# Hybrid decoder trunk with a hierarchical MoE: 16 KB weight rows, the head sums in a row, combines in four banks

## The chip, the cores and the metric

The kernel runs on one NeuronCore of one Trainium2 chip. The metric is the device time of one execution in microseconds (us). Engines are named as the profile names them: PE (matmuls; PEld is its weight load), DVE, ACT, POOL, and SP, which issues the DMAs.

## What is computed

The reference is a two-layer trunk on 512 tokens of width 1024, all in float32. Layer 0 mixes tokens with sliding-window attention (8 query heads, 2 key/value heads of 64) beside a gated delta rule; layer 1 with retention. After each follows a mixture of experts: 32 experts, each token goes to 2 of one group's 8.

```python
def attn_delta_mixer(h, pos, w_in, ...):
    aq, ak, av, bqkv, bz, ba, bb = _split(h @ w_in, EVEN_SPLITS)
    q = rms_norm(aq.reshape(bsz, s, SWA_Q_HEADS, SWA_HEAD_DIM), q_gain)
    k = rms_norm(ak.reshape(bsz, s, SWA_KV_HEADS, SWA_HEAD_DIM), k_gain)
    y_a = sliding_window_attention(partial_rope(q, pos), partial_rope(k, pos), v, sinks)
...
def expert_block(args):                       # in hierarchical_moe
    xb, e = args
    hid = jax.nn.silu(xb @ w_gate[e]) * (xb @ w_up[e])
    return hid @ w_down[e]
...
for layer in range(DEPTH):
    x = x + mixer(rms_norm(x, ...), ...)      # attn_delta_mixer, then retention_mixer
    x = x + hierarchical_moe(rms_norm(x, ln_ffn[layer]), ...)
```

w_gate and w_up of an expert are 1024 x 512, w_down is 512 x 1024: 2 MB each, 6 MB for an expert, and every expert's weights are read in both layers.

## The kernel before, in words

Each engine's program is written out by hand, and engines wait for each other by semaphores. The residual stream X stays in SBUF as 4 tiles of 128 tokens. PSUM is used as eight banks of 128 x 512 float32, PB[0] to PB[7]. Weights pass through a ring of six slots of 2 MB.

**Attention, in layer 0.** `attn_pe` computes the projections, then four products for the delta rule's first head and one for its second (`gproj_pe`, n = 0 to 4, 24 matmuls each), which need the weights split into an upper and a lower part; POOL makes the lower part for n = 0 to 3, DVE (`split_gdn_lower`, L422) for n = 4, after the loop that follows. In `attn_dve` DVE goes through the four token tiles: it sums the squares of every head (L597), waits for POOL, which makes rstd of it (L570, L571 in `attn_pool`), and then scales and rotates q and k of that tile (L605 to L615). In the second tile it also copies the convolution's weights (L600) and clears three columns (L603), for which ACT waits at L694. The four rotated tiles are then transposed on PE (L467).

**Experts.** Experts are taken in pairs, 16 pairs a layer, 64 token slots for each expert of a pair, so that the two work in the two halves of PE's columns. For pair i the six slots hold gate, up and down of both experts; `experts_sp` loads each matrix of the next pair as soon as PE has used up the one before it (L2102). In `experts_pe` pair(i) does this work, in this order:

- gate(i) and up(i): 64 matmul records at L1712, into PB[0] and PB[1];
- combine(i - 1): the rows of the pair before are brought back to the tokens, as eight sums of 128 x 512 (m = 0 to 7), two matmuls each (L1730), each added to X on DVE (L2014). The sums go into BC, PB[6] and PB[7], in turn;
- gather(i + 1): the tokens of the next pair are picked by a one-hot product (L1683), 8 matmuls for each half, into PB[0] and PB[1];
- hidden_t(i): four transposes (L1717) of the product of SiLU(gate) and up, which DVE makes at L1742 when up is done;
- x_transposed(i + 1): four transposes for each half (L1688), and slots_transposed(i + 1), four more (L1697);
- down(i): 32 matmul records at L1723, into BY, PB[4] and PB[5]. ACT and DVE take them out as an upper and a lower part (L1735, L1739).

combine is cut into four pieces of two sums between the others. A sum may start when the add of the sum two before it is done:

```python
                    if not (is_at(i, 0) and m < 2):
                        pe.wait_ge(*mw("added", 8 * i + m - 1))
                    comb_mm(pe, comb_bank(m), m, b).then_inc(ms("comb"), 1)
```

Pairs 2 to 13 are a loop in the program, pairs 0, 1, 14 and 15 are written out. The last pair's sums go through all eight banks (`LAST_ORDER`) and are added at L2019. On DVE pair(i) makes one-hots, the hidden product, six adds, x_out(0) (L1692, which takes the transposed tokens out of PSUM), two adds, x_out(1), and the lower part of y.

Of the kernel before, what the change touches and what calls it, by code (L numbers as in the profile page):

```python
# [26 lines left out]
NT = SEQ // P  # L27
# [3 lines left out]
RING = 6  # L31
# [62 lines left out]
def program(nc, x, ln_mix_even, w_in_even, conv_w_even, a_log_even, dt_bias_even, q_gain_even, k_gain_even,  # L94
# [8 lines left out]
    with ctx:  # L103
# [469 lines left out]
        def attn_dve(dve, step):  # L573
# [18 lines left out]
            for t in range(NT):  # L592
                v = QKv[:, t, :].rearrange("p (h d) -> p h d", d=ADH)
                x1, x2 = v[:, :, 0:8], v[:, :, 8:16]
                rot = [rt[:, a, t * 80:(t + 1) * 80].rearrange("p (h d) -> p h d", d=8) for a in range(4)]
                dve.wait_ge(sg("a_sq"), t + 1)
                dve.tensor_reduce(a_ss[:, t * AQK:(t + 1) * AQK], sq_tmp[:, t, :].rearrange("p (h d) -> p h d", d=ADH), AX, ALU.add).then_inc(sg("a_sums"), 1)  # L597
                if t == 1:
                    dve.wait_ge(sg("d_cw"), 1)
                    dve.tensor_copy(cw, PB[2][:, 0:48]).then_inc(sg("d_conv_ready"), 1)  # L600
                    dve.wait_ge(sg("d_conv_ready"), 1)
                    dve.wait_ge(sg("a_proj"), 8)
                    dve.memset(xc[:, :, 0:3], 0.0).then_inc(sg("d_conv_ready"), 1)  # L603
                dve.wait_ge(sg("a_rstd"), t + 1)
# [1055 lines left out]
        def comb_bank(m):  # L1660

            return BC[m % 2]

# [107 lines left out]
        def experts_pe(pe, l):  # L1771
# [21 lines left out]
            def down(i):  # L1793
                for u in range(2):
                    pe.wait_ge(*w_need(l, 4 + u, i))
                if not is_at(i, 0):
                    pe.wait_ge(*mw("y_lower", 2 * i))
                pe.wait_ge(*mw("ht_out", i + 1))
                for half in range(2):
                    down_mm(pe, half, range(2), w_two(l, 4, 4)).then_inc(ms("y"), 1)  # L1800

            def combine(i, b, ms_):
                for m in ms_:
                    if m == 0:
                        pe.wait_ge(*mw("y_lower", 2 * i + 2))
                        pe.wait_ge(*mw("ot_out", i + 1))
                    if not (is_at(i, 0) and m < 2):
                        pe.wait_ge(*mw("added", 8 * i + m - 1))
                    comb_mm(pe, comb_bank(m), m, b).then_inc(ms("comb"), 1)
# [23 lines left out]
            def pair(i, b):  # L1833
# [4 lines left out]
                if before:  # L1838
                    combine(i - 1, 1 - b, (0, 1))
                if more:  # L1840
                    gather(i + 1, 0)
                hidden_t(i)
                if before:
                    combine(i - 1, 1 - b, (2, 3))
                if more:
                    gather(i + 1, 1)
                if before:
                    combine(i - 1, 1 - b, (4, 5))
                if more:
                    x_transposed(i + 1, 0)  # L1850
                if before:
                    combine(i - 1, 1 - b, (6, 7))
                if more:
                    slots_transposed(i + 1)
                    x_transposed(i + 1, 1)
# [115 lines left out]
        def experts_dve(dve, l, step):  # L1971
# [54 lines left out]
            def pair(i, b):  # L2026
# [11 lines left out]
                hidden(i, b)  # L2038
                adds(i - 1, range(6))
                if more:  # L2040
                    x_out(i + 1, 0)
                adds(i - 1, (6, 7))
                if more:
                    x_out(i + 1, 1)
# [50 lines left out]
        def experts_sp(sp, l):  # L2095
            mats = (w_gate[l], w_up[l], w_down[l])

            def load(i, q):
                c = c_moe[l] + q
                sp.wait_ge(*(released[c - RING] if is_at(i, 0) else freed(l, q, i)))  # L2100
                src = mats[q // 2].rearrange("e (p k) n -> p e (k n)", p=P)[:, one(2 * i + q % 2), :]
                sp.dma_start(slot_of(c), src.rearrange("p e n -> p (e n)"), max_dma_last_dim=4096).then_inc(w_landed[c % RING], 16)  # L2102

# [6 lines left out]
        def overflow_sp(sp, l):  # L2110
# [4 lines left out]
            with sp.If(n_most > SLOTS):  # L2115
                sp.wait_ge(*mw("y", NE))
                with sp.Fori(1, SEQ // SLOTS) as b:
                    with sp.Fori(0, PAIRS) as i:
                        n = (b - 1) * PAIRS + i
                        for q, name in enumerate(("v_g0", "v_g1", "v_u0", "v_u1", "v_y0", "v_y1")):  # L2120
                            src = (w_gate[l], w_up[l], w_down[l])[q // 2].rearrange("e (p k) n -> p e (k n)", p=P)[:, bass.ds(2 * i + q % 2, 1), :]
                            sp.dma_start(w_over(l), src.rearrange("p e n -> p (e n)"), max_dma_last_dim=4096).then_inc(ms("v_w"), 16)
                            sp.wait_ge(*over_wait(l, name, n))
# [513 lines left out]
```

## Time and profile before

| | |
|---|---|
| median of 3 runs | 1770.93 us (1770.86 to 1772.2) |
| the profiled execution | 1770.01 us, its span 1768.1 us |
| PE busy | 1730.7 us, 98% |
| DVE, ACT, POOL busy | 659.0 (37%), 444.8 (25%), 212.2 us (12%) |
| read from HBM | 457 MB, 260 GB/s over the span |
| DMA in the experts' slices | 408 to 410 GB/s |
| experts, layer 0 and layer 1 | about 341 to 839 us and 1267 to 1765 us |
| chain of waits: PE, DVE, DMA | 91%, 3%, 2% |

PE's busy time in this profile covers the time in which matmuls follow one another with modelled ends, so 98% doesn't say that each matmul runs at its shortest. The chain of waits says what each stretch was spent on; the windows say what the DMA engines moved in it.

### The profile page before, as it was taken

The page shows a single profiled execution, that of the slowest core. Times are in us where ns is not written, and L with a number is a line of the kernel's source. Part 1 is how long each engine was busy: PE and PEld are TensorE (multiplying, and loading weights), DVE is VectorE, ACT ScalarE, POOL GpSimd, SP SyncE. Part 2 cuts the span into 40 slices and gives each one's busy share as a digit, 9 for nine tenths or more (in the row PEclk, how much of TensorE's full clock was granted, in tenths as well). Part 3 has the DMA queues.
Part 4 walks back from the last instruction along what each step waited for, and adds up shares of the span by engine and source line. Part 5 has one row for each costly group of instructions (what it writes and reads, how often), then busy time and mean ns, then how long its engine had stood idle before and what let it go on. Part 6 is the DMA issues. An engine that isn't in the chain of part 4 may idle for free.

```text
span 1768.1 us, 23453 instructions
## 1 busy us (share of the span) xinstructions
PE 1730.7 (98%) x9323; PEld 1106.5 (63%) x9323; DVE 659.0 (37%) x1164; ACT 444.8 (25%) x868; POOL 212.2 (12%) x152
## 2 busy tenths in 40 slices
PE   7899999999999999999999999999999999999998
PEld 6778988754444545454988888888754544445453
DVE  3775764423232323234413223132522332323233
ACT  4365653311111111112342322323311111111110
POOL 2400100100000000001533442442000000000000
PEclk9999999999999999999999999999999999999999
DMA  8410112599999999999122222122499999999996
GB/s 196 100 48 1 49 51 96 189 408 409 409 409 410 409 410 409 410 409 364 49 72 83 84 95 96 48 96 95 191 393 409 410 409 410 410 410 409 410 409 243
DMA packets 141177, 460.39 MB, mean 260 GB/s; under 512 B 5552, under 2 KB 31376, under 8 KB 140208
## 3 DMA queue, kind: packets, MB, share of 16 engines
q1 hardware_dynamic: 140368, 457.01, 66.5%
q0 software_dynamic: 736, 2.34, 1.1%
q8 instruction: 54, 0.88, 0.2%
q14 instruction: 19, 0.16, 0.0%
HBM read 457.24 MB, written 2.10 MB: 260 GB/s over the span
## 4 chain that ended last, share of the span: by engine, by line
PE 91%; DVE 3%; DMA 2%; ACT 1%; SPq 1%; issue 1%; POOL 0%; DVEq 0%; ACTq 0%
PE bank L153 28%; PE bank L1712 25%; PE bank L1723 12%; PE bank L1730 7%; PE bank L1683 7%; PE bank L1688 2%; DMA ring<-in_w_in_even_dram 1%; PE bank L2240 1%; DMA ring<-in_w_in_odd_dram 1%; PE bank L1717 1%; SPq L2487 1%; PE bank L1478 1%; PE bank L1697 1%; PE bank L927 1%; PE bank L914 1%
## 5 line engine op out<-in xcount | busy, mean ns | idle before, releaser
L1712 PE MATMUL bank<-ring,SCR 128*64 128x512 f32 x2048 | 448.9, 593 | 1.6 <-DVE SCR L1692 0.9
L153 PE MATMUL bank<-ring_r 128*128 128x512 f32 (+2 forms) x1216 | 359.8, 378 | 10.0 <-DVE ring_r L422 5.1
L1712 PEld LDWEIGHTS bank<-ring,SCR 128*64 128x64 f32 x2048 | 152.6, 137 | 291.6 <-issue 284.5
L153 PEld LDWEIGHTS bank<-ring_r 128*128 128x128 f32 x1216 | 225.5, 192 | 52.2 <-DVE ring_r L422 5.5
L2171 POOL TENSOR_TENSOR ring_r<-ring,ring_r 128x1024 fp32r<-128x1024 f32 x62 | 150.7, 2463 | 707.2 <-DVE ring_r L2171 482.7
L1723 PE MATMUL bank<-ring,SCR 128*64 128x512 f32 x1024 | 226.8, 595 | 0.0
L2014 DVE TENSOR_TENSOR X<-X,bank 128x512 f32<-128x512 f32 x240 | 153.9, 682 | 96.1 <-PE bank L1730 96.0
L1742 DVE SCALAR_TENSOR_TENSOR SCR<-SCR,bank 128x512 f32<-128x512 f32 x32 | 23.9, 748 | 360.8 <-PE bank L1712 360.8
L1730 PE MATMUL bank<-SCR_r 128*128 128x512 f32 x512 | 152.5, 419 | 1.6 <-DVE SCR_r L1739 0.9
L1723 PEld LDWEIGHTS bank<-ring,SCR 128*64 128x64 f32 x1024 | 70.6, 137 | 132.3 <-issue 128.7
L153 PE MATMUL bank<-ring_r,SCR_r 128*128 128x512 f32 x576 | 138.7, 395 | 0.0
L1919 ACT COPY SCR<-bank 128x512 f32<-128x512 f32 x64 | 37.5, 587 | 352.8 <-PE bank L1683 352.8
L153 PE MATMUL bank<-ring_r,HT_r 128*128 128x512 f32 (+1 forms) x320 | 121.3, 379 | 0.0
L1730 PEld LDWEIGHTS bank<-SCR_r 128*128 128x128 f32 x512 | 86.4, 189 | 54.3 <-issue 25.1
L153 PEld LDWEIGHTS bank<-ring_r,SCR_r 128*128 128x128 f32 x576 | 106.5, 188 | 22.0
L1739 DVE TENSOR_TENSOR SCR_r<-bank,SCR_r 128x512 fp32r<-128x512 f32 x64 | 44.3, 692 | 194.9 <-ACT SCR_r L1735 194.9
L153 PE MATMUL bank<-HT_r,ring_r 128*128 128x512 f32 (+1 forms) x288 | 107.6, 374 | 0.0
L2164 ACT CAST ring_r<-ring 128x1024 fp32r<-128x1024 f32 x64 | 62.4, 1050 | 96.2 <-PE bank L153 89.4
L1735 ACT CAST SCR_r<-bank 128x512 fp32r<-128x512 f32 x64 | 37.5, 585 | 195.3 <-PE bank L1723 195.3
L1683 PE MATMUL bank<-HT_r,SCR_r 128*128 128x512 f32 x256 | 69.8, 394 | 0.0
L1939 ACT ACTIVATE SCR<-bank 128x512 f32<-128x512 f32 x32 | 19.1, 597 | 199.5 <-PE bank L1712 199.5
L1683 PE MATMUL bank<-XN_r,SCR_r 128*128 128x512 f32 x256 | 68.7, 390 | 0.0
(413 smaller groups left out, 1710.0 us busy)
## 6 DMA issues: line engine op xcount, KB each, us to landing
ring<-in_w_gate_dram SPq DMA_DIRECT2D x64, 2048.0 KB, 15.1
ring<-in_w_up_dram SPq DMA_DIRECT2D x64, 2048.0 KB, 18.4
ring<-in_w_down_dram SPq DMA_DIRECT2D x64, 2048.0 KB, 15.3
ring<-in_w_in_odd_dram SPq DMA_DIRECT2D x8, 2048.0 KB, 8.9
ring<-in_w_in_even_dram SPq DMA_DIRECT2D x16, 512.0 KB, 6.7
ring<-in_w_in_odd_dram SPq DMA_DIRECT2D x8, 1024.0 KB, 8.0
ring<-in_w_out_odd_dram SPq DMA_DIRECT2D x4, 2048.0 KB, 7.5
ring<-in_w_out_even_dram SPq DMA_DIRECT2D x2, 2048.0 KB, 8.2
```

Source lines behind the costliest of these rows:

```text
L153: mm = pe.matmul(out, lhs[a], rhs[b], start=(first and i == 0), stop=(last and i == 2))
L1683: mm = pe.matmul(BX[half][:, :], OH[:, t, :], part[:, t, half * 512:(half + 1) * 512], start=(t + i == 0), stop=(t == NT - 1 and i == 1))
L1688: mm = pe.transpose(BX[g][:, j * P:(j + 1) * P], XG[:, g * 512 + j:(g + 1) * 512:4], ident)
L1712: mm = pe.matmul(bank[SLOTS * u:SLOTS * u + SLOTS, :], x_tile(k, u), w[u][:, k, :], start=(k == 0), stop=(k == KT - 1))
L1723: mm = pe.matmul(BY[half][SLOTS * u:SLOTS * u + SLOTS, :], HHT[:, j * P + SLOTS * u:j * P + SLOTS * u + SLOTS], w[u][:, j, half * 512:(hal ...
L1730: mm = pe.matmul(bank[:, :], OT[b][:, t * P:(t + 1) * P], part[:, half * 512:(half + 1) * 512], start=(i == 0), stop=(i == 1))
L1735: return act.copy(YU[:, half * 512:(half + 1) * 512], BY[half][:, :])
L1739: return dve.tensor_tensor(YL[o], BY[half][:, :], YU[o].bitcast(F32), ALU.subtract)
L1919: act.copy(XG[:, half * 512:(half + 1) * 512], BX[half][:, :]).then_inc(ms("xg"), 1)
L2014: dve.tensor_tensor(x_part(m), x_part(m), comb_bank(m)[:, :], ALU.add).then_inc(ms("added"), 1)
L2164: act.copy(WU[j % 2][:, at], slot_of(c)[:, at]).then_inc(sg("r_upper"), 1)
L2171: eng.tensor_tensor(ring_r[:, c % RING, at], slot_of(c)[:, at], WU[j % 2][:, at].bitcast(F32), ALU.subtract).then_inc(sg("r_lower"), 1)
```

## The change

Three edits.

1. The experts' weight loads no longer say `max_dma_last_dim=4096`. A load is 128 rows of 16 KB, which was cut into elements of 4 KB and is now moved as 16 KB elements.
2. In `attn_dve` the four sums of squares stand in a row, with the copy and the clearing behind them, and the scaling and rotation of the four tiles follow in a second loop.
3. In the experts the sums go through four banks, PB[6], PB[7], PB[4], PB[5]; a sum waits for the add of the sum four before it, and down waits for the adds of sums 6 and 7, as it writes PB[4] and PB[5]. The sums are done in two pieces of four. The twelve transposes for the next pair stand together ahead of down. On DVE the eight adds stand together ahead of both x_out.

```diff
             for t in range(NT):
-                v = QKv[:, t, :].rearrange("p (h d) -> p h d", d=ADH)
...
                 dve.wait_ge(sg("a_sq"), t + 1)
                 dve.tensor_reduce(a_ss[:, t * AQK:(t + 1) * AQK], sq_tmp[:, t, :].rearrange("p (h d) -> p h d", d=ADH), AX, ALU.add).then_inc(sg("a_sums"), 1)
                 if t == 1:
                     dve.wait_ge(sg("d_cw"), 1)
                     dve.tensor_copy(cw, PB[2][:, 0:48]).then_inc(sg("d_conv_ready"), 1)
-                    dve.wait_ge(sg("d_conv_ready"), 1)
-                    dve.wait_ge(sg("a_proj"), 8)
-                    dve.memset(xc[:, :, 0:3], 0.0).then_inc(sg("d_conv_ready"), 1)
+            dve.wait_ge(sg("d_conv_ready"), 1)
+            dve.wait_ge(sg("a_proj"), 8)
+            dve.memset(xc[:, :, 0:3], 0.0).then_inc(sg("d_conv_ready"), 1)
+            for t in range(NT):
+                v = QKv[:, t, :].rearrange("p (h d) -> p h d", d=ADH)
...
                 dve.wait_ge(sg("a_rstd"), t + 1)
                 step.then(dve.tensor_tensor(v, v, a_rs[...], ALU.mult))
...
         def comb_bank(m):
-            return BC[m % 2]
+            return (BC + BY)[m % 4]
...
                 for half in range(2):
+                    if not is_at(i, 0):
+                        pe.wait_ge(*mw("added", 8 * i - 1 + half))
                     down_mm(pe, half, range(2), w_two(l, 4, 4)).then_inc(ms("y"), 1)
...
-                    if not (is_at(i, 0) and m < 2):
-                        pe.wait_ge(*mw("added", 8 * i + m - 1))
+                    if not (is_at(i, 0) and m < 4):
+                        pe.wait_ge(*mw("added", 8 * i + m - 3))
                     comb_mm(pe, comb_bank(m), m, b).then_inc(ms("comb"), 1)
...
                 if before:
-                    combine(i - 1, 1 - b, (0, 1))
+                    combine(i - 1, 1 - b, range(4))
                 if more:
                     gather(i + 1, 0)
                 hidden_t(i)
-                if before:
-                    combine(i - 1, 1 - b, (2, 3))
                 if more:
                     gather(i + 1, 1)
                 if before:
-                    combine(i - 1, 1 - b, (4, 5))
+                    combine(i - 1, 1 - b, range(4, 8))
                 if more:
                     x_transposed(i + 1, 0)
-                if before:
-                    combine(i - 1, 1 - b, (6, 7))
-                if more:
                     slots_transposed(i + 1)
                     x_transposed(i + 1, 1)
                 down(i)
...
                 hidden(i, b)
-                adds(i - 1, range(6))
+                adds(i - 1, range(8))
                 if more:
                     x_out(i + 1, 0)
-                adds(i - 1, (6, 7))
-                if more:
                     x_out(i + 1, 1)
                 y_out(i)
...
-                sp.dma_start(slot_of(c), src.rearrange("p e n -> p (e n)"), max_dma_last_dim=4096).then_inc(w_landed[c % RING], 16)
+                sp.dma_start(slot_of(c), src.rearrange("p e n -> p (e n)")).then_inc(w_landed[c % RING], 16)
```

**PE, pair 1 of layer 0, from up's end to down.** L1712 is gate and up, L1730 the sums, L1683 the gather, L1717 hidden_t, L1688 and L1697 the transposes for the next pair, L1723 down. Before:

```order
L1730 MATMUL bank<-SCR_r 128x512 x4
L1683 MATMUL bank<-HT_r,SCR_r 128x512 x4
L1683 MATMUL bank<-XN_r,SCR_r 128x512 x4
L1717 MATMUL bank<-CE,SCR 128x128 x4
L1730 MATMUL bank<-SCR_r 128x512 x4
L1683 MATMUL bank<-HT_r,SCR_r 128x512 x4
L1683 MATMUL bank<-XN_r,SCR_r 128x512 x4
L1730 MATMUL bank<-SCR_r 128x512 x4
L1688 MATMUL bank<-CE,SCR 128x128 x4
L1730 MATMUL bank<-SCR_r 128x512 x4
L1697 MATMUL bank<-CE,SCR 128x128 x4
L1688 MATMUL bank<-CE,SCR 128x128 x4
```

And with the change, in which each of these lines has a number one higher:

```order
L1731 MATMUL bank<-SCR_r 128x512 x8
L1684 MATMUL bank<-HT_r,SCR_r 128x512 x4
L1684 MATMUL bank<-XN_r,SCR_r 128x512 x4
L1718 MATMUL bank<-CE,SCR 128x128 x4
L1684 MATMUL bank<-HT_r,SCR_r 128x512 x4
L1684 MATMUL bank<-XN_r,SCR_r 128x512 x4
L1731 MATMUL bank<-SCR_r 128x512 x8
L1689 MATMUL bank<-CE,SCR 128x128 x4
L1698 MATMUL bank<-CE,SCR 128x128 x4
L1689 MATMUL bank<-CE,SCR 128x128 x4
```

The same 16 matmuls of the sums now stand in two groups of 8 in place of four of 4, and nothing of them stands between the transposes.

**SP, the load of one pair in the loop of layer 0.** Before:

```order
L2102 DMA ring<-in_w_gate_dram 128x4x1024
L2102 ISA
L2102 DMA ring<-in_w_gate_dram 128x4x1024
L2102 DMA ring<-in_w_up_dram 128x4x1024 x2
L2102 DMA ring<-in_w_down_dram 128x4x1024 x2
```

With the change:

```order
L2098 DMA ring<-in_w_gate_dram 128x4096
L2098 ISA
L2098 DMA ring<-in_w_gate_dram 128x4096
L2098 DMA ring<-in_w_up_dram 128x4096 x2
L2098 DMA ring<-in_w_down_dram 128x4096 x2
```

The same six loads in the same places, each with 128 elements of 4096 floats in place of 512 of 1024.

**DVE, layer 0's attention, from the first sum on.** Before, one tile's turn and the next sum stand like this (the sum is L597):

```order
L605 TENSOR_TENSOR SCR<-SCR 128x640
L606 TENSOR_TENSOR SCR<-SCR 128x640
L609 TENSOR_TENSOR SCR<-SCR,CE 128x80
L610 TENSOR_TENSOR SCR<-SCR,CE 128x80
L611 TENSOR_TENSOR SCR<-SCR,CE 128x80
L612 TENSOR_TENSOR SCR<-SCR,CE 128x80
L614 TENSOR_TENSOR SCR<-SCR 128x10x8
L615 TENSOR_TENSOR SCR<-SCR 128x10x8
L597 TENSOR_REDUCE SCR<-SCR 128x10
L600 COPY SCR<-bank 128x48
L603 MEMSET ring 128x3x3
```

With the change, the sums (L594) stand ahead of the first tile's turn:

```order
L597 COPY SCR<-bank 128x48
L594 TENSOR_REDUCE SCR<-SCR 128x10 x2
L600 MEMSET ring 128x3x3
L606 TENSOR_TENSOR SCR<-SCR 128x640
L607 TENSOR_TENSOR SCR<-SCR 128x640
```

No sum stands between two tiles' turns any more, and no tile's turn stands between a sum and the next.

## Rows read from the trace of the kernel before

**Rows 1.** The page's chain of waits, by engine.

```profile
PE 91%; DVE 3%; DMA 2%; ACT 1%; SPq 1%; issue 1%; POOL 0%; DVEq 0%; ACTq 0%
```

**Rows 2.** Chain of waits in time: gates of pairs 1, 10, 15, layer 1's 1, 15.

```profile
375.18 13.73 PE bank L1712 x64
...
650.59 13.95 PE bank L1712 x64
...
804.10 6.89 PE bank L1712 x32
...
1301.41 13.73 PE bank L1712 x64
...
1729.97 6.87 PE bank L1712 x32
```

**Rows 3.** Windows: us; PE, PEld, DVE, ACT, POOL busy; PE clock, DMA share, GB/s.

```profile
500.00:550.00 50.00, 50.00 (x235) 25.72 (x232) 14.84 (x25) 6.38 (x12) 0.00 (x0) 1.00 1.03 410
```

**Rows 4.** DMA issues of a window from 527 us: size in KB, us to landing.

```profile
ring<-in_w_up_dram SPq DMA_DIRECT2D x2, 2048.0 KB, 20.7
```

**Rows 5.** Windows, while one load of w_out_odd, 128 rows of 16 KB, runs.

```profile
1174.00:1178.00 4.00, 4.00 (x20) 3.30 (x19) 3.97 (x4) 2.25 (x3) 4.00 (x3) 1.00 1.01 430
```

**Rows 6.** The page's DMA issues: KB, us from issue to landing.

```profile
ring<-in_w_out_odd_dram SPq DMA_DIRECT2D x4, 2048.0 KB, 7.5
```

**Rows 7.** Chain of waits in time, one pair (3) of layer 0: start, us, what.

```profile
436.12 13.73 PE bank L1712 x64
449.85 1.12 PE bank L1730 x4
...
453.29 0.93 PE bank L1730 x4
...
456.05 0.91 PE bank L1730 x4
...
457.43 1.27 PE bank L1730 x4
...
466.63 13.73 PE bank L1712 x64
```

**Rows 8.** The same view, pair 0 of layer 0, which has no sums.

```profile
364.88 1.85 PE bank L1683 x8
```

**Rows 9.** PE and DVE in order of time: the first sums of a pair.

```profile
603.03 1.20 PE L1730 MATMUL bank<-SCR_r 128*128 128x512 f32 x4
...
603.90 1.28 DVE L2014 TENSOR_TENSOR X<-X,bank 128x512 f32<-128x512 f32 x2
```

**Rows 10.** Chain of waits in time, last pair of layer 1; then DVE there.

```profile
1743.99 1.13 PE bank L1730 x4
...
1749.90 7.04 PE bank L1723 x32
...
1744.80 1.28 DVE L2014 TENSOR_TENSOR X<-X,bank 128x512 f32<-128x512 f32 x2
```

**Rows 11.** Attention: PE in order of time, then the chain of waits in time.

```profile
77.97 0.80 PE L153 MATMUL bank<-ring_r 128*128 128x512 f32 x1 [5.06 <-DVE ring_r L422]
...
77.97 8.32 PE bank L153 x24
...
133.56 5.54 PE bank L153 x24
```

**Rows 12.** Windows in that stretch (columns as in rows 3).

```profile
80.00:82.00 2.00, 2.00 (x7) 1.54 (x6) 2.00 (x3) 0.00 (x0) 0.00 (x0) 0.50 1.20 272
```

**Rows 13.** DVE in order of time, attention: second tile, third sum and turn.

```profile
61.69 0.82 DVE L605 TENSOR_TENSOR SCR<-SCR 128x640 f32<-128x640 f32 x1 [2.14 <-POOL SCR L571]
...
64.45 0.81 DVE L597 TENSOR_REDUCE SCR<-SCR 128x10 f32<-128x640 f32 x1
...
67.63 0.82 DVE L605 TENSOR_TENSOR SCR<-SCR 128x640 f32<-128x640 f32 x1 [2.37 <-POOL SCR L571]
```

**Rows 14.** ACT in order of time at the end of layer 0's experts.

```profile
827.74 1.99 ACT L2164 CAST ring_r<-ring 128x1024 fp32r<-128x1024 f32 x2 [6.75 <-DMA ring<-in_w_in_odd_dram]
```

More of the change, by code:

```diff
@@ L592, in attn_dve @@
             for t in range(NT):
-                v = QKv[:, t, :].rearrange("p (h d) -> p h d", d=ADH)
-                x1, x2 = v[:, :, 0:8], v[:, :, 8:16]
-                rot = [rt[:, a, t * 80:(t + 1) * 80].rearrange("p (h d) -> p h d", d=8) for a in range(4)]
                 dve.wait_ge(sg("a_sq"), t + 1)
@@ L600, in attn_dve @@
                     dve.tensor_copy(cw, PB[2][:, 0:48]).then_inc(sg("d_conv_ready"), 1)
-                    dve.wait_ge(sg("d_conv_ready"), 1)
-                    dve.wait_ge(sg("a_proj"), 8)
-                    dve.memset(xc[:, :, 0:3], 0.0).then_inc(sg("d_conv_ready"), 1)
+            dve.wait_ge(sg("d_conv_ready"), 1)
[3 more added lines that the diff above has]
+                v = QKv[:, t, :].rearrange("p (h d) -> p h d", d=ADH)
+                x1, x2 = v[:, :, 0:8], v[:, :, 8:16]
+                rot = [rt[:, a, t * 80:(t + 1) * 80].rearrange("p (h d) -> p h d", d=8) for a in range(4)]
                 dve.wait_ge(sg("a_rstd"), t + 1)
@@ L2121, in overflow_sp @@
                             src = (w_gate[l], w_up[l], w_down[l])[q // 2].rearrange("e (p k) n -> p e (k n)", p=P)[:, bass.ds(2 * i + q % 2, 1), :]
-                            sp.dma_start(w_over(l), src.rearrange("p e n -> p (e n)"), max_dma_last_dim=4096).then_inc(ms("v_w"), 16)
+                            sp.dma_start(w_over(l), src.rearrange("p e n -> p (e n)")).then_inc(ms("v_w"), 16)
                             sp.wait_ge(*over_wait(l, name, n))
```

## The prediction

> **What bounds the kernel now.** I read the chain of waits first. It is PE for 91% [rows 1], so time is won only where PE is held up or where its own sequence gets shorter. Both happen in two places: the experts, 28 nearly equal pairs, and one gap in the attention.
>
> In the experts the starts of the gates give a pair's length. From pair 1 to pair 15 layer 0 takes 804.10 - 375.18 = 428.92 us, layer 1 1729.97 - 1301.41 = 428.56 us [rows 2]: 857.5 us for 28 pairs, 30.62 each. They aren't all alike. In the middle gate and up take 13.95 us and a pair (804.10 - 650.59) / 5 = 30.70; at the start of a layer gate and up take 13.73 [rows 2]. The difference of 0.22 us is a wait for weights. A pair needs six loads of 2,097,152 bytes, 12.58 MB; in 30.70 us that is 410 GB/s, and the windows show a flat 410 with the DMA engines' share at 1.03 [rows 3]. The up weights take 20.7 us from issue to landing [rows 4], where a load alone takes 7.5 [rows 6]: PE is a little faster than the stream, and the queue's delay has grown until PE stops for it, at the start of up. So PE and DMA are within 1% of each other: speeding up either alone meets the other at once.
>
> A pair that doesn't wait for DMA is, piece by piece [rows 7]: gate and up 13.73, sums 1.12 + 0.93 + 0.91 + 1.27 = 4.23, and the rest (gathers, transposes, down) unchanged below. Such a pair lasts 466.63 - 436.12 = 30.51 us.
>
> In the attention PE stands still for 5.06 us ahead of the product n = 4, whose lower weights DVE makes at L422 [rows 11]. The 24 matmuls behind the gap take 8.32 us; the same 24 later take 5.54 [rows 11]. In that stretch the granted clock is 0.50, the lower level of 1.2 GHz [rows 12]; it fell in PE's gap. DVE comes late to L422 as it waits in each of four tiles for POOL's rstd: 2.14 and 2.37 us idle in the two tiles shown, and as much in the others [rows 13].
>
> **The 16 KB elements.** Six loads, same bytes, same places. What 16 KB elements give is bounded by two rows: the present stream, 410 [rows 3], as the case in which nothing changes, and the 430 GB/s of a load of w_out_odd, which is moved so already [rows 5]. I take 430, as it is the same kind of load on the same queue; then the stream needs 12.58 MB / 430 = 29.3 us for a pair. PE needs more than that (next part), so all waits for weights in the pairs go, about 0.2 us in each pair of the second half of a layer, and the stream has 0.9 us to spare. Below nothing: a load of this kind alone takes 7.5 us to land [rows 6], of which 4.9 are movement; this would hurt if it weren't overlapped with the next (a rival).
>
> The Trainium skill, DMA: Bandwidth & Descriptors, section Specifications, says that transfers of 512 B and more run at line rate. By that rule 4 KB elements lose nothing, and this edit gives 0; rows 3 and 5, 410 against 430, speak against it, though the second is one load at a time. The same page's fabric ceiling of 435 GB/s leaves room for 430.
>
> **The sums, in two groups of 8.** In a row of matmuls of this kind four cost 0.91 us, 0.2275 each [rows 7]. First group, after up: 1.12 + 0.91 = 2.03. Second group, after the gather: 8 x 0.2275 = 1.82. Together 3.85 against 4.23: 0.38 less, most of it the wait for an add in the last group (1.27 against 0.91). The gather that now follows hidden_t costs 0.03 more (1.85 after transposes in pair 0 [rows 8], against 1.82). I take 0.35: a pair of 30.51 - 0.35 = 30.16 us. Bounds: 30.51 (the switch costs only move) and 30.0 (switches cheaper than read).
>
> The new waits. Sum 4 waits for the add of sum 0. DVE's adds start 0.87 us after the first group (603.90 against 603.03, where PE starts it) and take 0.64 each [rows 9]: the four are done at 3.4, and the second group starts only at 2.03 + 1.82 + 1.85 and 0.5 of hidden_t, at 6.2. Down waits for the add of sum 6. With the same delay from a group's start to its first add, adds 4 to 6 are done by 6.2 + 0.87 + 3 x 0.64 = 9.0; down is reached at 6.2 + 1.82 and 1.4 of transposes (the rest of the pair: 466.63 - 457.43 - 1.27 is 7.9 with only two of the three), at 9.4. That is 0.4 us to spare, thin, but down's second half, which needs add 7 (9.6), comes 3.5 us later. x_out ends near 11.0 and the next gate is at 16.4; nobody waits for it. Neither wait costs anything as long as adds take 0.64.
>
> 28 pairs: 857.5 - 28 x 30.16 = 857.5 - 844.5 = **13.0 us**.
>
> **The last pair of each layer** has no gathers to hide adds, and takes 1749.90 - 1743.99 = 5.91 us from up to down. Now: group 2.04, hidden_t about 0.5, second group at once; DVE starts its adds at 0.81 [rows 10], four are done by 3.4, the seventh, which down waits for, at 3.5 + 3 x 0.64 = 5.4. 0.45 us less, twice: **0.9 us**.
>
> **The end of layer 0's experts.** ACT waits there 6.75 us for layer 1's first weights [rows 14], which stand in the queue behind the experts'. Without the backlog they land earlier. I cost it at nothing; at most 1 us is to be had, since down ends only afterwards.
>
> **The attention.** The four sums in a row take 4 x 0.81 us. A sum and POOL's answer take 67.63 - 64.45 = 3.2 us, a tile's turn 64.45 - 61.69 = 2.8 [rows 13]: now a tile costs 6.0. In a row, the last three sums run while POOL makes its first answer, so the first turn starts when it did; POOL's further answers come every 2.4 us at most, faster than DVE's turns. Three times 3.2 us goes, less what the copy and short waits keep. The four turns end about 9 us earlier and the split at L422, which released PE at 77.97, about 69. PE needs it at 77.97 - 5.06 = 72.9. The gap of 5.06 us goes, and with it the clock's fall: 8.32 - 5.54 = 2.78 us. **7.8 us** together; if the clock fell all the same it would be 5.1. Late next is nothing near: DVE moves 9 us and PE 7.8, so DVE's convolutions behind the rotations are still ahead of PE's scores, by 1 us more than before. The clearing at L603 comes earlier too, which frees ACT at L694; it had time. Everything behind is tied to PE and moves with it.
>
> **Sum.** 13.0 + 0.9 + 7.8 = 21.7 us. The profiled execution took 1770.0 (span 1768.1 and 1.9 around it), 0.9 under the median of the runs: 1748.3 by it, 1749.2 by the median. I say 1748.5.
>
> **Rivals.**
> 1. *The stream stays at 410* (the 430 holds for one load alone). PE gets faster and only waits more for up: the end of a layer's pairs is set by the stream, which runs without a pause in both, so the 13.0 go. 1770.0 - 7.8 - 0.9 = 1761.3. For it: 410 is flat to the last digit. Against it: rows 5. This is also what the rule that the Trainium skill gives in DMA: Bandwidth & Descriptors would have.
> 2. *The stream gets faster, the new order gives nothing* (down waits for the adds, or the switch costs return elsewhere). 28 x 30.51 = 854.3, 3.2 less, and 7.8: 1759.0. For it: the 0.4 us to spare for add 6.
> 3. *Slower: loads of 16 KB elements don't overlap in a row.* One alone takes 7.5 us to land for 4.9 of movement [rows 6]. It decides where a load's turn in the queue costs more than 5.17 us (now 5.12, 30.70 / 6, plus what the attention gives back, spread over 180 loads). If only 0.8 of the 2.6 remained between loads, a pair would take 6 x 5.7 = 34.2, and 30 pairs 105 us more: about 1867. Against it: within that load the share is 1.01 [rows 5], and the present loads follow each other at 410 without a dip [rows 3].
> 4. *The rotations gain but the clock falls elsewhere*: 5.1 in place of 7.8, 1751.0. Part of the likeliest case's range.
>
> That the change doesn't do what it says is out for the elements and the order, as the instructions' shapes and places show.
>
> **Chances.** The forecast with rival 4 has 0.74, and 1743.5 to 1754 as its own range (a pair of 30.0 to 30.3, the attention 5.1 to 8). Rival 2 has 0.10, rival 1 0.10, rival 3 0.04, something that cancels all of it 0.02. The range takes in rival 2: 1743.5 to 1759.0, which leaves out 0.16 and little at the edges. A measurement of this kernel tells 0.2%, 3.5 us, from no change. Faster 0.94, same 0.02, slower 0.04.
>
> **What would show it.** Right: gates 30.1 to 30.2 us apart from pair 1 to 15 in both layers, GB/s in the experts' slices at 416 to 418 with the DMA share under 1, up's landing shorter than 20.7 and not growing, sums of 2.0 and 1.8 us in two groups, no gap of PE at 73 to 78 us and no clock of 0.50 there. Wrong: gates 30.7 apart (rival 1); 30.5 with down held by L2012's adds (rival 2); PE idle for weights in every pair (rival 3).

## The result, and the profile after

The changed kernel takes 1750.42 us (median of 4 runs, 1746.16 to 1754.61), the one before beside it 1770.91: a ratio of 0.9886 with a 95% interval of 0.9874 to 0.9898, and by the medians 20.5 us less. The prediction said 1748.5 and a range of 1743.5 to 1759.0.

The profiled execution is the slowest of the four, 1754.61 us, its span 1752.8; the one before had 1768.1. So this pair of traces shows 15.3 us of difference, and the chain of waits in time says where. The starts of the gates give the first three columns (of before [rows 2]); the last column is a second profiled execution of the changed kernel (e5 below), span 1746.8.

| stretch | before | after | difference | after again, difference |
|---|---|---|---|---|
| start to the gate of pair 1, layer 0 | 375.18 | 375.76 | +0.58 | -5.43 |
| pair 1 to pair 15, layer 0 | 428.92 | 422.13 | -6.79 | -6.79 |
| pair 15 to pair 1 of layer 1 | 497.31 | 495.57 | -1.74 | -1.75 |
| pair 1 to pair 15, layer 1 | 428.56 | 422.13 | -6.43 | -6.43 |
| gate of pair 15 to the end | 38.13 | 37.21 | -0.92 | -0.90 |
| sum | 1768.1 | 1752.8 | -15.3 | -21.3 |

Four rows are the same in both executions to 0.02 us. The first is not: of the 7.8 us that the attention was to give, nothing is left at that point in one execution and 5.4 us in the other, beside this one execution of before; what more executions show stands under rival 4 below.

The chain of waits in time, after; the gates of the same pairs as [rows 2] (start, us, what):

```profile
375.76 13.73 PE bank L1713 x64
...
797.89 13.73 PE bank L1713 x64
...
1293.46 13.73 PE bank L1713 x64
...
1715.59 13.73 PE bank L1713 x64
```

422.13 us for 14 pairs is 30.15 a pair in both layers. No gate and up takes more than 13.73, and at pair 15 the chain no longer breaks off after the gate [rows 2]: the wait for the up weights is gone. The same view, one pair, where [rows 7] showed four pieces of sums:

```profile
556.66 13.73 PE bank L1713 x64
570.40 2.04 PE bank L1731 x8
...
576.59 1.82 PE bank L1731 x8
578.41 0.47 PE bank L1689 x4
...
579.80 7.02 PE bank L1724 x32
586.82 3.43 PE bank L1713 x15
```

The sums take 2.04 + 1.82 = 3.86 us for 4.23 before. In the rows left out the gathers take 1.83 and 1.85 and hidden_t 0.47; the three transposes start at 578.41, 578.88 and 579.32, nothing stands between them and the next piece, and down follows the last transpose at once. The window that answers to [rows 3], with the same columns:

```profile
500.00:550.00 50.00, 50.00 (x242) 26.10 (x240) 15.96 (x26) 7.07 (x14) 0.00 (x0) 1.00 1.00 420
```

The stream moved 420 GB/s here with the share at 1.00. And lines of the page after: the chain by engine (before [rows 1]), the group of down's matmuls (busy us, mean ns, idle before and who ended it), and one of its DMA issues (KB, us to landing):

```profile
PE 96%; DVE 2%; ACT 1%; issue 1%; DMA 0%; POOL 0%; DVEq 0%; ACTq 0%; POOLq 0%
...
L1724 PE MATMUL bank<-ring,SCR 128*64 128x512 f32 x1024 | 226.8, 595 | 1.7 <-DVE X L2012 1.7
...
ring<-in_w_up_dram SPq DMA_DIRECT2D x64, 2048.0 KB, 15.7
```

PE is 96% of the chain where it was 91%, and DMA's 2% are gone. The up weights land 15.7 us after their issue, for 18.4 in the page before. L1724 is down: over all 32 pairs it waited 1.7 us for adds, and the last pair of each layer accounts for nearly all of that. It is the only new wait that the experts show. The chain in the last pair of layer 1, which answers to [rows 10]:

```profile
1729.32 2.05 PE bank L1731 x8
...
1731.84 1.86 PE bank L1731 x8
...
1733.72 0.69 DVE X L2012
...
1734.55 7.10 PE bank L1724 x32
```

From up to down 5.23 us for 5.91. With the issue around it 0.85 us of it are spent on an add (1733.70 to 1734.55).

In the attention the gap of PE [rows 11] is gone; DVE's split at L422 starts at 69.59 instead of at about 76.7, and PE had work until then. But DVE in order of time shows a wait that was forecast to be none (its answer to [rows 13]; the bracket is the idle time and who ended it):

```profile
59.39 0.83 DVE L606 TENSOR_TENSOR SCR<-SCR 128x640 f32<-128x640 f32 x1 [0.70 <-POOL SCR L571]
...
69.59 1.22 DVE L422 TENSOR_TENSOR ring_r<-ring,ring_r 128x1024 fp32r<-128x1024 f32 x1
```

The four turns start at 55.85, 59.39, 62.93 and 66.45. One takes 3.54 us, not 2.8: DVE waits 0.7 us for POOL in three of the tiles. POOL in order of time, after, says why. The first answer is made while DVE adds up squares, the others while it scales and rotates:

```profile
53.53 0.21 POOL L570 TENSOR_SCALAR SCR<-SCR 128x10 f32<-128x10 f32 x1 [0.86 <-DVE SCR L594]
53.83 1.99 POOL L571 TENSOR_TENSOR SCR<-SCR,mhalf 128x10 f32<-128x10 f32 x1
55.90 0.85 POOL L570 TENSOR_SCALAR SCR<-SCR 128x10 f32<-128x10 f32 x1
56.84 2.52 POOL L571 TENSOR_TENSOR SCR<-SCR,mhalf 128x10 f32<-128x10 f32 x1
```

The same two instructions take 2.2 us beside the sums and 3.4 beside the turns.

### The profile page after: what moved, and what is told of

The parts are those of the page before. It is cut to its first block, busy times and chain, and to the rows that moved or that the text cites. A ratio compares the mean times of both kernels' runs of the same rounds, so it can differ in the third digit from the quotient of the medians.

```text
span 1752.8 us, 23471 instructions
## 1 busy us (share of the span) xinstructions
PE 1719.3 (98%) x9323; PEld 1110.8 (63%) x9323; DVE 654.8 (37%) x1164; ACT 445.6 (25%) x868; POOL 215.8 (12%) x152
## 4 chain that ended last, share of the span: by engine, by line
PE 96%; DVE 2%; ACT 1%; issue 1%; DMA 0%; POOL 0%; DVEq 0%; ACTq 0%; POOLq 0%
PE bank L153 32%; PE bank L1713 25%; PE bank L1724 13%; PE bank L1731 7%; PE bank L1684 7%; PE bank L1689 2%; PE bank L2236 1%; PE bank L1718 1%; PE bank L1479 1%; PE bank L1698 1%; PE bank L503 1%; PE bank L928 1%; PE bank L915 1%; PE bank L480 1%; PE bank L931 1%
## 5 line engine op out<-in xcount | busy, mean ns | idle before, releaser
L1724 PE MATMUL bank<-ring,SCR 128*64 128x512 f32 x1024 | 226.8, 595 | 1.7 <-DVE X L2012 1.7
L2012 DVE TENSOR_TENSOR X<-X,bank 128x512 f32<-128x512 f32 x240 | 148.5, 681 | 97.2 <-PE bank L1731 97.1
L1724 PEld LDWEIGHTS bank<-ring,SCR 128*64 128x64 f32 x1024 | 71.6, 137 | 133.2 <-issue 129.6
L1731 PE MATMUL bank<-SCR_r 128*128 128x512 f32 x512 | 131.5, 399 | 0.5 <-DVE SCR_r L1740 0.5
L1731 PEld LDWEIGHTS bank<-SCR_r 128*128 128x128 f32 x512 | 93.3, 188 | 45.5 <-issue 26.0
## 6 DMA issues: line engine op xcount, KB each, us to landing
ring<-in_w_up_dram SPq DMA_DIRECT2D x64, 2048.0 KB, 15.7
```

Source lines behind the costliest of these rows:

```text
L1724: mm = pe.matmul(BY[half][SLOTS * u:SLOTS * u + SLOTS, :], HHT[:, j * P + SLOTS * u:j * P + SLOTS * u + SLOTS], w[u][:, j, half * 512:(hal ...
L1731: mm = pe.matmul(bank[:, :], OT[b][:, t * P:(t + 1) * P], part[:, half * 512:(half + 1) * 512], start=(i == 0), stop=(i == 1))
L2012: dve.tensor_tensor(x_part(m), x_part(m), comb_bank(m)[:, :], ALU.add).then_inc(ms("added"), 1)
```

## The experiments

**Theory A** is the prediction's: the 16 KB elements lift the stream above what PE asks for, the order takes 0.35 us out of every pair, and the sums in a row close PE's gap in the attention. The other theories are the rivals, as each expectation names them. The kernel before, beside e1 to e4, took 1770.36 us (21 runs, 1766.91 to 1775.1); beside e5, e6, e7 and e9 1771.88 (9 runs); beside e8, e10 and e11 1771.19 (15 runs).

### Each edit alone

**e1: the kernel before, with 16 KB elements only.**

```diff
-                sp.dma_start(slot_of(c), src.rearrange("p e n -> p (e n)"), max_dma_last_dim=4096).then_inc(w_landed[c % RING], 16)
+                sp.dma_start(slot_of(c), src.rearrange("p e n -> p (e n)")).then_inc(w_landed[c % RING], 16)
```

> The kernel before with edit 1 alone, the 16 KB elements. Theory A (at 4 KB the weight stream ends at 410 GB/s and holds PE up by 0.2 us a pair; 16 KB elements lift that end): every pair from 1 to 15 lasts 30.5 us in both layers, gate and up 13.73, up's landing well under 20.7 us, and the median is 3 to 4 us lower, about 1767. Theory B (the stream was no bound, all of the gain is the order on PE): no change, 1770.9, some gates and ups still at 13.95.

Measured: 1766.53 us, ratio 0.9981 (0.9972 to 0.9991), 3.8 us less by the medians. A pair of the second half of layer 0, in the chain:

```profile
650.98 13.73 PE bank L1712 x64
...
672.29 1.27 PE bank L1730 x4
...
681.49 0.85 PE bank L1712 x3
```

Its sums, 1.12, 0.93, 0.91 and 1.27, are those of before [rows 7], its gate and up take 13.73 where they took 13.95 [rows 2], and the pair takes 30.51: what a pair of before takes where no weights are late. So the elements give the waits for weights and no more.

**e2: the order in the experts only, 4 KB elements.**

```diff
-            return BC[m % 2]
+            return (BC + BY)[m % 4]
...
-                    combine(i - 1, 1 - b, (0, 1))
+                    combine(i - 1, 1 - b, range(4))
...
-                    combine(i - 1, 1 - b, (4, 5))
+                    combine(i - 1, 1 - b, range(4, 8))
```

> The kernel before with edit 3 alone, four banks and the new order, elements at 4 KB. Theory A: PE would do a pair in 30.15 us, but the stream needs 30.7, so gates are 30.7 apart nearly from the start and the median falls by about 1 us only (the last pairs), to 1770. Theory B (the order alone carries the gain): gates 30.15 apart and 1757.

Measured: 1769.96 us, ratio 0.9998 (0.9988 to 1.0008). The chain, and a window of the same execution:

```profile
455.84 22.97 DMA ring<-in_w_up_dram
...
478.95 7.10 PE bank L1712 x32
...
509.67 7.10 PE bank L1712 x32
```

```profile
500.00:550.00 50.00, 49.32 (x231) 22.79 (x228) 14.91 (x25) 5.30 (x10) 0.00 (x0) 1.00 1.03 410
```

The chain now goes through the weights, and up starts 0.14 us after they land: 30.72 us from one up to the next, at the old 410 GB/s. PE has become faster, waits for the difference, and the order alone is worth nothing.

**e4: elements and order together**, the edits of e1 and e2 in one kernel.

> The changed kernel without edit 2, so edits 1 and 3 together. Theory A: gates 30.15 apart, 13 us from the pairs and 0.9 to 1.5 from the last pairs and the end of layer 0, 1757 to 1756.5, all runs within 1.5 us as before's, since the attention is before's. More than edits 1 and 3 give one by one (3.5 and 1). Theory B (edits add up): about 1766.

Measured: 1757.47 us, ratio 0.9923 (0.9909 to 0.9936), 12.9 us less by the medians, with gates 30.15 apart (466.94 and 497.09 in the chain). The five runs spread over 3.5 us, where 1.5 was expected. The two edits give 3.8 and 0.4 us by the medians when alone, and 12.9 together. This is the signature of two limits within 1% of each other: each edit lifts one of them, and the kernel moves only as far as the other.

**e3: the sums of the attention in a row only.** Its edit is the part of the change's diff that stands in `attn_dve`; the core of it:

```diff
+            for t in range(NT):
+                v = QKv[:, t, :].rearrange("p (h d) -> p h d", d=ADH)
```

> The kernel before with edit 2 alone, the head sums in a row. Theory A: the gap of 5.06 us of PE and the fall of the clock in it go, 7.8 us, 1763, less what clock falls at other places take back, which differ from run to run: runs spread over 5 us and more, between 1762 and 1771, and each run's time goes with its mean clock. Theory B (the spread of the changed kernel comes from the experts' edits): runs within 1 us of each other.

Measured: 1764.28 us, ratio 0.9962 (0.9949 to 0.9976), 6.1 us less, where 7.8 less what other falls of the clock take was expected. Its five runs spread over 4.3 us and follow their mean clocks (0.996 at 1761.4 us, 0.994 at 1765.72). DVE waits the same 0.69 us for POOL in three tiles, and the scores start at 81.60, as in e5 below. With e4 the product of the ratios is 0.9885; the whole change measured 0.9886. Between the experts and the attention nothing is lost or gained that these intervals could show.

### What in the order makes a pair shorter

**e9: the changed kernel, with the sums in their four old places**, in four banks.

```diff
-                    combine(i - 1, 1 - b, range(4))
+                    combine(i - 1, 1 - b, (0, 1))
...
+                    combine(i - 1, 1 - b, (2, 3))
...
-                    combine(i - 1, 1 - b, range(4, 8))
+                    combine(i - 1, 1 - b, (4, 5))
...
+                    combine(i - 1, 1 - b, (6, 7))
```

> The changed kernel with the sums in four banks but in the old places: four pieces of two sums, transposes and x_out as before. Theory A (the gain of the order on PE is the wait for the adds of two banks, 0.36 us in the last piece; the grouping itself gives nearly nothing, 0.02): pieces of 1.13, 0.93, 0.91 and 0.91 to 0.93, gates 30.15 to 30.2 apart. Theory B (the gain is fewer switches between kinds of matmul): gates 30.4 and more apart.

Measured: 1748.81 us, one execution. The chain of one pair:

```profile
459.44 13.73 PE bank L1713 x64
473.18 1.12 PE bank L1731 x4
...
480.76 0.93 PE bank L1731 x4
...
489.62 2.57 PE bank L1713 x11
```

Three pieces are those of before (1.12, 0.93, 0.91), and the last has lost its wait: 0.93 for 1.27. The pair takes 30.18, within 0.03 of the grouped one. So the four banks carry the gain; doing the sums four in a row and the transposes together is worth 0.03 us a pair, 0.8 us in all, which the time of one execution can't show.

### What the elements do to the stream

In the changed kernel PE is the slower side, so its stream cannot show its own limit. Three kernels make PE faster than any stream: they leave the lower part of y out of the sums, 8 matmuls where there were 16, so that the residual lacks it, and differ in the size of the elements.

```diff
-            for i, part in enumerate((YU, YL)):
-                mm = pe.matmul(bank[:, :], OT[b][:, t * P:(t + 1) * P], part[...], start=(i == 0), stop=(i == 1))
+            for i, part in enumerate((YU,)):
+                mm = pe.matmul(bank[:, :], OT[b][:, t * P:(t + 1) * P], part[...], start=True, stop=True)
```

**e6: 16 KB elements.**

> The changed kernel with only the upper part of y in the sums, so half of their matmuls are left out. PE's work in a pair falls by 8 x 0.2275 = 1.8 us, to 28.3. Theory A (a stream of 16 KB elements ends near 430 GB/s): the stream bounds now, gates 29.2 to 29.4 apart, 428 to 431 GB/s. Rival (the stream has no end near there, or only at the fabric's 435): 28.9 or 28.3 apart.

**e7: 4 KB elements** (`max_dma_last_dim=4096` again).

> The same with elements of 4 KB. Theory A: gates stay at 30.7 apart and 410 GB/s, though PE has 1.8 us less to do. Rival (410 was only what PE asked for): 29.3 or less apart.

**e8: 8 KB elements** (`max_dma_last_dim=8192`).

> As the run with only the upper part of y in the sums, with elements of 8 KB. The stream bounds, so the gates tell what it gives. At 4 KB a pair took 30.72 us for 3072 elements, 192 on each of the 16 DMA engines, at 16 KB 29.37 for 48 on each: 1.35 us for 144 elements, 9.4 ns for each element beside its bytes. Theory A (a fixed price for each element): at 8 KB, 96 on each, 29.37 + 48 x 0.0094 = 29.82 apart, 422 GB/s. Rival (a threshold between 4 and 16 KB): 29.37 or 30.72.

Measured: 1728.81, 1764.29 and 1737.12 us, one execution each. The chain of e6, of e7 and of e8, two ups in a row (start, us, what):

```profile
464.20 7.10 PE bank L1713 x32
...
493.59 7.10 PE bank L1713 x32
```

```profile
496.26 7.10 PE bank L1713 x32
...
526.98 3.50 PE bank L1713 x9
```

```profile
461.06 7.10 PE bank L1713 x32
...
490.90 7.10 PE bank L1713 x32
```

And one window of each, in the same order:

```profile
500.00:550.00 50.00, 49.23 (x238) 24.26 (x236) 19.57 (x32) 7.65 (x15) 0.00 (x0) 1.00 1.01 429
```

```profile
500.00:550.00 50.00, 47.93 (x224) 23.97 (x222) 17.34 (x28) 7.05 (x14) 0.00 (x0) 0.97 1.03 410
```

```profile
500.00:550.00 50.00, 48.11 (x233) 22.82 (x231) 17.69 (x30) 8.24 (x16) 0.00 (x0) 1.00 1.01 422
```

All three are bound by the stream: a pair takes 29.4 us with 16 KB elements (29.37 from the next up to the one after), 30.72 with 4 KB, 29.84 with 8 KB; 429, 410 and 422 GB/s. In e7's window the granted clock is 0.97, and yet the spacing is that of e2 at 1.00. A pair has 3072 elements of 4 KB, 192 for each of 16 DMA engines, or 96 of 8 KB, or 48 of 16 KB. The first halving saves 0.88 us for 96 elements, 9.2 ns each; the second 0.47 us for 48, 9.8 ns each. So an element costs about 9.5 ns besides its bytes. Taking all of them away would leave 29.37 - 48 x 0.0095 = 28.9 us, or 435 GB/s, an estimate. The Trainium skill, DMA: Bandwidth & Descriptors, gives 435 GB/s as the fabric's ceiling in its Specifications, and the long windows agree: none of 50 us moved more than 430 (e6). Windows of 1 and 2 us can't test it, as single ones show up to 475 (893 to 894 us before) beside lower ones. Its line there that transfers of 512 B and more run at line rate does not hold to the accuracy that this kernel needs: 4 KB elements lose 4.5% against 16 KB.

### The clock in the attention

**e10: the kernel before, with 22 matmuls of no use in PE's gap**, into the bank that the product n = 4 then overwrites.

```diff
+                if n == 4:
+                    g_left_bank(pe, 1)
+                    for j in range(22):
+                        pe.matmul(g_bank(4)[:, :], HTU0[:, j % KT, 0:P], HTU0[:, j % KT, :], start=True, stop=True)
```

> The kernel before, with 22 more matmuls (128 x 512, their results written over) on PE in its gap of 5.06 us in the attention. They don't release anything: PE still waits for DVE's L422 until about 78 us. Theory A (the clock falls because PE stands still, and this costs 2.8 us of the edit's gain): no clock of 0.50 at 77 to 84 us, the 24 matmuls behind take 5.5 us in place of 8.3, and the median is 2 to 3 us lower, 1768. Theory B (the clock falls there for another reason, or would have fallen later anyway): no change in the median.

Measured: 1769.58 us, ratio 0.999 (0.9979 to 1.0): 1.6 us less, where 2 to 3 was expected, at the edge of what can be told. The chain, and the window of [rows 12]:

```profile
16.81 35.15 PE bank L153 x192
...
74.65 4.99 PE bank L461 x22
79.63 5.46 PE bank L153 x24
...
88.83 1.71 PE bank L484 x16
```

```profile
80.00:82.00 2.00, 2.00 (x11) 1.65 (x10) 1.93 (x4) 0.00 (x0) 0.00 (x0) 1.00 1.17 216
```

The 24 matmuls take 5.46 us for 8.32 [rows 11] at a clock of 1.00 for 0.50 [rows 12]. Filling the gap with work is enough; nothing needs to arrive earlier. The filler (L461) takes 4.99 us and would have ended at about 77.9, no later than the 24 matmuls began before (77.97). They begin 1.66 us later here for another reason: this execution had a fall of the clock at 18 to 22 us (0.57), in which the first 192 matmuls took 35.15 us for 33.61 in e5, and PE came to the filler at 74.65, where it began its gap at 72.9 before. So the net at the scores (L484), 88.83 for 90.04 before, holds 1.2 of the 2.8 us. Every trace says the same of this place: in the four profiled executions with the gap (before, e1, e2, e4) the clock of 80 to 82 us is 0.50 to 0.55, in the nine without it 1.00. The fall of the clock there was PE's gap, as the prediction had it.

**e5: the changed kernel again**, unchanged, on another chip than e1 to e4.

> The changed kernel once more, beside the kernel before on the same chip. Theory A (times of single runs are the program's time plus what clock falls cost, in both kernels): the median is 1750 to 1751, the runs of both kernels spread over some 8 us, and within each kernel a run's time falls with its mean clock, about 1.4 us for each 0.001. Theory B (the spread has another source): no such order by the clock.

Measured: 1747.81 us (5 runs, 1746.07 to 1753.26), ratio 0.9868 (0.985 to 0.9885): 2 to 3 us under the 1750 to 1751 expected, with the spread (7.2 us) and the order by the mean clock as expected. The chain of e5 and then of the first profile of the changed kernel, the attention:

```profile
81.71 1.71 PE bank L480 x16
...
98.91 5.54 PE bank L153 x24
```

```profile
83.30 1.71 PE bank L480 x16
...
101.27 7.92 PE bank L153 x24
```

The scores start 8.3 us earlier than before (90.04) in e5, and 6.7 earlier in the other. Windows of that other execution:

```profile
18.00:22.00 4.00, 4.00 (x24) 4.00 (x24) 4.00 (x9) 4.00 (x6) 3.93 (x6) 0.63 1.15 304
100.00:104.00 4.00, 4.00 (x13) 3.42 (x14) 1.75 (x4) 2.12 (x4) 0.00 (x0) 0.50 0.01 4
180.00:184.00 4.00, 4.00 (x21) 4.00 (x21) 1.91 (x4) 0.63 (x1) 3.57 (x4) 0.50 0.00 0
```

The granted clock was at its lower level, 1.2 GHz, in the last two, as in one of 200 to 204 us, and partly in the first. In e5 all four of these windows are at 1.00; its falls come at other places, the first of them at 174 to 178 us (0.66). The fall at 20 us costs the 1.6 us between 83.30 and 81.71; the one at 101 makes 24 matmuls take 7.92 us for 5.54, another 2.4, and 0.8 in the 16 ahead of them (L503, 2.53 for 1.73). That is 4.8 of the 6.0 us between the two at the gate of pair 1; the falls at 180 and 200 us cost the rest more than e5's own falls did.

### A version with other banks in the last pair

**e11: other banks for the sums in the last pair**, so that neither they nor down wait for adds. They go through PB[6], 7, 3, 0, 1, 6, 7, 3; the three in PB[3], PB[0], PB[1] wait until DVE and ACT have read these banks out, and down waits for the adds of the pair before only.

```diff
+            return PB[(6, 7, 3, 0, 1, 6, 7, 3)[m]] if end else (BC + BY)[m % 4]
...
+                    end = is_at(i, last - 1)
+                    if end and 2 <= m < 5:
+                        pe.wait_ge(*mw(("gs_out", "sil", "hh")[m - 2], last + 1))
+                    elif end and m >= 5:
+                        pe.wait_ge(*mw("added", 8 * i + m - 4))
```

> The changed kernel with other banks for the sums in the last pair of each layer alone: PB[6], 7, 3, 0, 1, 6, 7, 3, all free there, so that down need not wait for the adds of sums 6 and 7. Theory A (down waits there for the seventh add, 0.85 us, twice): from up's end to down 4.4 us in place of 5.2, 1.7 us less in all, 1748 if the changed kernel is at 1749.5; too little for a verdict, so the chain decides. Rival (the adds then hold up the last sums behind down): the stretch from up to the end of the layer stays as long.

Measured: 1745.42 us (4 runs, 1744.41 to 1746.61), ratio 0.9853 (0.9838 to 0.9868). The chain of the last pair of layer 1:

```profile
1720.46 2.05 PE bank L1731 x8
...
1724.82 7.04 PE bank L1724 x32
```

4.36 us from up to down for 5.23 in the changed kernel and 5.91 before [rows 10], and in layer 0 the same (803.93 to 808.30). That is 0.87 us in each layer, 1.7 in all, which the trace shows; the rival, that the last sums then come later behind down, is out: from the gate of pair 15 to the end it is 36.27 us for 37.21 (table above). The medians differ by 2.4 us from e5's and 5.0 from the first, of which the rest is within the spread of the changed kernel. The interval of the ratio overlaps e5's (0.985 to 0.9885). So that it beats the kernel before is shown by the runs, and that it beats the changed kernel by the chain only.

## Why the prediction was right, point by point

- **What bounds the kernel: right.** PE and the stream within 1% of each other is what e1, e2 and e4 show together (3.8, 0.4 and 12.9 us).
- **The 16 KB elements: right, and the value taken was.** 430 was read from a load of its own [rows 5]; e6 streams at 429 without a pause. That they agree to 1 GB/s is in part luck: single microseconds of that load read 410 to 442. The time didn't depend on it, as any stream above the 417 that PE asks for gives the same. Rival 1 would have had 410 and 1761.3; e6 and e7 rule it out. The spare was 0.8 us a pair (30.15 - 29.37), forecast 0.9.
- **Rival 3, loads that don't overlap: out.** w_out_odd still takes 7.8 us to land alone by the page after, and the six loads of a pair land one behind the other at 429 GB/s.
- **The sums: 2.04 and 1.82 for 2.03 and 1.82; a pair 30.15 for 30.16.** 13.2 us for the 28 pairs, forecast 13.0. Most of it was said to be the wait for an add in the last piece; e9 shows that this is nearly all of it. The move of the transposes and the groups of four are 0.03 us a pair.
- **Down's wait for add 6: nothing**, as said, in the pairs with gathers. About 0.6 us was to spare where 0.4 was estimated: in the pair shown above the second four adds run from 577.17 to 579.65, the third of them to about 579.1, and down starts at 579.73. Rival 2's mechanism shows only in the last pairs.
- **The last pairs: 0.68 us each from up to down, forecast 0.45.** The wait that was named is there (0.69 of the add and 0.16 around it).
- **The wait for the last pair's own up weights: a term that the sum left out.** It counted the waits for weights from pair 1 to pair 15's gate and not the one inside pair 15. In layer 1 gate and up of pair 15 took 1743.99 - 1729.97 = 14.02 us [rows 2, 10] and take 13.73 now: 0.3. In layer 0 the up matmuls of before had a wait of 0.62 us for their weights (the row below); from the gate of pair 15 to down it was 20.41 us and is 18.96, of which 0.68 are the sums' and about 0.8 this wait.

```profile
811.59 7.09 PE L1712 MATMUL bank<-ring,SCR 128*64 128x512 f32 x32 [0.62 <-DMA ring<-in_w_up_dram]
```

- **The end of layer 0: 0.4 us, forecast 0 and at most 1.** ACT waits for layer 1's first weights for 3.0 us instead of 6.75 [rows 14], and from down's start to the sums behind it, it is 8.49 us in place of 8.87. With this, 1.74 us between the two layers' pairs are accounted for to 0.1, and 0.92 at the end of layer 1.
- **The attention: the mechanism was right, one step in it wrong, and the price depends on the execution.** The gap and the clock's fall in it are gone: 8.3 us at the scores in e5, forecast 7.8 (e10 and the thirteen traces above). The step that failed is "POOL's further answers come every 2.4 us at most, faster than DVE's turns": they come every 3.5 us, since POOL's two instructions take 3.4 beside DVE's turns. The duration was read where POOL ran beside an idle DVE. It costs DVE 3 x 0.7 us: the split at L422 was to release PE at about 69, 9 us earlier, and ended at 70.8 (69.59 + 1.22), 7 us earlier. It costs the kernel nothing, because PE needs it only at 72.9, when n = 3 is finished.
- **Rival 4, the clock falls elsewhere**, was taken as a minor case of 2.8 us. In the first profiled execution it took everything that the attention gave, in e5 2.9 us (5.4 of 8.3 were left at pair 1's gate). All profiled executions together say what the edit gives. Where the attention is the changed one, the gate of pair 1 starts at 366.01 (e3), 366.33 (e8), 367.22 (e7), 368.07 (e11), 368.94 (e9), 369.75 (e5), 370.84 (e6) and 375.76 us, the middle 368.5; where it is the old one, at 375.18, 376.36 (e1), 376.49 (e4) and 380.28 (e2), the middle 376.4. That is 7.9 us, as forecast, beneath a spread of 10 us. The runs' medians, 20.5 and in e5 24.1 us less, lie to both sides of the sum of 21.7, and the 1750.42 measured is nearer to this rival's 1751.0 than to 1748.5.
- **That the sum comes out so near is in part luck.** In e5's trace the two rows around the layers' ends give 2.65 us for the 0.9 forecast, and the attention 2.4 less than forecast: two misses that cancel, and 21.3 for 21.7.
- **The signs named in advance:** gates, sums, up's landing (17.6 in the window of [rows 4] for 20.7, and 15.8 to 16.3 in later ones) and the missing gap came as said; the GB/s were 420 in the window of 500 to 550 us and the DMA share 1.00, where 416 to 418 and a share under 1 were expected. 12.58 MB in 30.15 us is 417 over a pair; a window of 50 us cuts pairs in two.

## What to carry to other kernels

Where two resources are within 1% of each other, an edit to either is worth little alone and must be tried with the edit to the other: 3.8 and 0.4 us became 12.9. To read a stream's limit, make the other side faster on purpose and look at the spacing of its starts, as e6 to e8 do. When work is moved so that two engines run beside each other that took turns before, a duration read from the old trace may not hold; look for a place where the two already overlap.

## What the runs showed of the hardware that was not expected

- **An element of a DMA costs about 9.5 ns on its engine besides its bytes**, from 4 to 16 KB, in a stream of 12.58 MB a pair (410, 422, 429 GB/s).
- **POOL is slowed by some of DVE's work.** L570 takes 0.21 us beside the sums of squares and 0.84 beside L606; L571 takes 1.99 and 2.52; DVE's own instructions keep their 0.83. L606 and L607 read two operands from SBUF, the sums (L594) one. The Trainium skill, GPSIMD Engine Reference, section Specifications, has POOL's access to SBUF shared with DVE and in contention with instructions of two SBUF inputs; the trace agrees, 0.84 for 0.21. In three tiles L570 starts 0.05 us behind the start of L606 and ends 0.06 to 0.07 behind its end (56.75 and 56.68 us in the first), as if it waited for it. No experiment here separated the operands from the other differences.
- **The clock falls in places that change from one execution to the next.** At 180 to 184 us it was 0.50 with PE busy for 4.00 of 4.00 us by the records, whose ends are modelled. What PE did ahead of these falls can be read: before the one at 100 us it was busy for 0.79 of the 2 us from 96 to 98, and all falls between 170 and 210 us, in every profiled execution, set in within or less than 3 us behind one of two groups of 32 matmuls of a single column each (128x1), which the records count as busy. Not each of these groups has a fall: e3's first has none. The same 32 matmuls (L855 before, L856 after) took 3.47 us at 198.76 before, 4.63 at 196.39 after and 4.41 at 190.03 in e5. The runs follow it: e5's five had mean clocks of 0.997, 0.996, 0.995, 0.995 and 0.992 and took 1746.07, 1746.18, 1747.81, 1748.6 and 1753.26 us. The kernel before spreads as widely, 1766.91 to 1775.1 in 21 runs. Whether these groups cause the falls is not shown, as no run changed them; e10 settles only the one at 78 us.
